# 22 sums of w_down quarters, made on VectorE before and by DRAM-to-DRAM transfers of GpSimd's queue after

## The reference

```
h = rms_norm(x);  proj = h @ w_in           # q, k, v, forget logits, pool input, conv x/B/C, gates
y_a = forgetting_attention(q, k, v) @ w_proj_attn      # 8 heads of 64, causal
y_b = multiscale_pool(u) @ w_proj_pool;  y_c = short_gated_conv(...) @ w_proj_conv
x = x + (gates[0]*y_a + gates[1]*y_b + gates[2]*y_c) @ w_out
a, b = split(rms_norm(x) @ w_gate_up)       # hidden 2816 each
x = x + (silu(a) * b) @ w_down              # w_down: 2816 x 1024: the "way down"
return rms_norm(x)
```

## Time and profile before

| | us |
|---|---|
| median of 3 runs | 773.13 |
| the profiled execution, its own time | 774.61 |
| its span | 772.8 |
| PE busy | 762.9 (99%) |
| DVE (VectorE) busy | 649.2 (84%) |
| ACT (ScalarE) busy | 420.6 (54%) |
| POOL (GpSimd) busy | 18.3 (2%) |
| granted TensorE clock | 0.998 of full speed |

### The profile page before, as it was taken

The page is one execution under the profiler, slowest core; times in us unless marked ns, Lnnn a source line. Parts: engine busy times, 40 slices in busy tenths (PEclk is TensorE's granted clock), DMA queues, the critical chain, the costliest instruction groups (busy, mean ns, idle before and its releaser), DMA issues.

```text
span 772.8 us, 12216 instructions
## 1 busy us (share of the span) xinstructions
PE 762.9 (99%) x4451; PEld 677.7 (88%) x4451; DVE 649.2 (84%) x1041; ACT 420.6 (54%) x712; POOL 18.3 (2%) x41
## 2 busy tenths in 40 slices
PE   8999999999999999999999999999999999999997
PEld 7888888888889999999978888999999998888885
DVE  6788876767798969777777899899999985799997
ACT  5626556647544546455445744555555552655554
POOL 2001101100000000000000000000000000000001
PEclk9999999999999999999999999999999999999999
DMA  8862542323133443344376533333333365353422
GB/s 296 271 220 76 174 105 69 91 54 100 42 105 82 110 121 98 83 110 113 106 265 198 192 98 93 110 111 109 97 100 106 110 196 159 128 172 122 151 96 110
DMA packets 133311, 99.46 MB, mean 129 GB/s; under 512 B 5932, under 2 KB 114532, under 8 KB 133252
## 3 DMA queue, kind: packets, MB, share of 16 engines
q1 hardware_dynamic: 132596, 98.35, 42.2%
q10 hardware_dynamic: 144, 0.26, 0.1%
q0 software_dynamic: 512, 0.07, 0.1%
HBM read 90.21 MB, written 8.39 MB: 128 GB/s over the span
## 4 chain that ended last, share of the span: by engine, by line
PE 96%; DVE 2%; issue 1%; DMA 1%; ACT 0%; POOL 0%; POOLq 0%; DVEq 0%
PE bank L913 10%; PE bank L917 10%; PE bank L915 10%; PE bank L1349 7%; PE bank L1347 7%; PE bank L1345 7%; PE bank L1161 4%; PE bank L1400 4%; PE bank L1159 4%; PE bank L1401 4%; PE bank L1399 4%; PE bank L1157 4%; PE bank L1195 2%; PE bank L1196 2%; PE bank L1197 2%; PE bank L1258 1%
## 5 line engine op out<-in xcount | busy, mean ns | idle before, releaser
L913 PE MATMUL bank<-operands,whi 128*128 128x512 f32 x352 | 138.2, 393 | 0.7 <-DVE wlo L2076 0.7
L917 PE MATMUL bank<-operands,wlo 128*128 128x512 f32 x352 | 137.3, 390 | 0.0
L915 PE MATMUL bank<-operands,whi 128*128 128x512 f32 x352 | 137.2, 390 | 0.0
L2076 DVE TENSOR_TENSOR wlo<-raw,whi 128x1024 fp32r<-128x1024 f32 x61 | 74.3, 1223 | 16.4 <-ACT whi L1465 15.7
L913 PEld LDWEIGHTS bank<-operands,whi 128*128 128x128 f32 x352 | 66.2, 188 | 14.3 <-DVE wlo L2076 1.1
L1465 ACT CAST whi<-raw 128x1024 fp32r<-128x1024 f32 x61 | 63.9, 1052 | 26.9 <-PE bank L917 8.3
L917 PEld LDWEIGHTS bank<-operands,wlo 128*128 128x128 f32 x352 | 66.1, 188 | 13.9
L915 PEld LDWEIGHTS bank<-operands,whi 128*128 128x128 f32 x352 | 66.2, 188 | 13.2
L1349 PE MATMUL bank<-sums_hi,wlo 128*128 128x256 f32 x240 | 68.0, 283 | 0.0
L1347 PE MATMUL bank<-sums_lo,whi 128*128 128x256 f32 x240 | 68.0, 283 | 0.0
L1345 PE MATMUL bank<-sums_hi,whi 128*128 128x256 f32 x240 | 68.0, 283 | 0.0
(11 more groups left out here) (323 smaller groups left out, 2001.8 us busy)
## 6 DMA issues: line engine op xcount, KB each, us to landing
raw<-in_w_in_dram SPq DMA_DIRECT2D x105, 256.0 KB, 3.3
raw<-in_w_gate_up_dram SPq DMA_DIRECT2D x88, 256.0 KB, 3.3
raw<-in_w_down_dram SPq DMA_DIRECT2D x53, 256.0 KB, 3.0
big_x<-in_x_dram SPq DMA_DIRECT2D x8, 512.0 KB, 5.0
tiles<-in_w_out_dram SPq DMA_DIRECT2D x4, 1024.0 KB, 7.4
w_sums<-tiles SPq DMA_DIRECT2D x4, 1024.0 KB, 7.2
raw<-w_sums SPq DMA_DIRECT2D x16, 256.0 KB, 3.1
raw<-in_w_out_dram SPq DMA_DIRECT2D x12, 256.0 KB, 3.7
```

What stands on the lines that cost most here:

```text
L913: nc.tensor.matmul(banks[b][:, 0:width], whi[:, s, w], op(hi + k * S), start=a, stop=False)
L915: nc.tensor.matmul(banks[b][:, 0:width], whi[:, s, w], op(lo + k * S), start=False, stop=False)
L917: mm = nc.tensor.matmul(banks[b][:, 0:width], wlo[:, s, w], op(hi + k * S), start=False, stop=z)
L2076: nc.vector.tensor_tensor(wlo[:, s, :], raw[:, s, :], whi[:, s, :].bitcast(F32), ALU.subtract).then_inc(w_lo, 1)
```

## The change

A new DRAM tensor `down_sums` holds 22 sums: kind 0 is B12 + B11 and kind 1 is B11 + B21 for every r. GpSimd's queue makes them during the pair passes, each kind in two transfers of 1408 rows of 2 KB (2.88 MB): in pass 0 it copies the first addend of kind 0 to DRAM, in pass 1 it waits for that copy and adds the second addend by an accumulating DMA; passes 2 and 3 do the same for kind 1. The transfers stand behind the 4 small DMAs of their pass in the queue. VectorE's `first_sum` and the first addition of `second_sums` are gone. SP waits for both adding transfers ahead of its first w_down load, and loads the sums in place of the second block: kind 0 straight into `chain(r)`, kind 1 into the raw slot. The number and size of its loads stay. For this the load of r = 3 now waits until `used` reaches NU (before, that wait stood in VectorE's `first_sum(3)` and at the load of r = 6). ScalarE waits for the landing in place of VectorE's sum.

```diff
+        down_sums = nc.dram_tensor("down_sums", [2 * FH // 2, D // 2], F32, kind="Internal").ap()
+        def down_sum(kind):
+            return down_sums[kind * R * P:(kind + 1) * R * P, :]
 ... SP
+            sp.wait_ge(down_added, 32)
             for r in range(R):
-                if r == SPARE:
+                if r == SLOTS:
                     sp.wait_ge(used, NU)
-                elif r == SPARE + SLOTS:
+                if r == SPARE + SLOTS:
                     sp.wait_ge(w_lo, NU + 2 * (SPARE - SLOTS) + 2)
-                else:
+                elif r != SPARE:
                     sp.wait_ge(w_lo, NU - SLOTS + r + 1 if r < SLOTS else NU + 2 * (r - SLOTS) + 2)
                 sp.sem_inc(loads_begun, 1)
-                load_down(r, [(2 * r, 1), (2 * r, 0)])
+                load_down(r, [(down_block(2 * r, 1), down_raw(r, 0)),
+                              (down_sum(0)[r * P:(r + 1) * P, :], chain(r))])
...
-                load_down(R + r, [(2 * r, 0), (2 * r + 1, 0)])
+                load_down(R + r, [(down_sum(1)[r * P:(r + 1) * P, :], down_raw(R + r, 0)),
+                                  (down_block(2 * r + 1, 0), down_raw(R + r, 1))])
 ... GpSimd, at the end of each pass i of its loop over the pairs
+                kind, adds = i // 2, i % 2
+                down = w_down.rearrange("(r e p) c -> p r e c", e=2, p=P)
+                to = down_sum(kind).rearrange("(r p) c -> p r c", p=P)
+                if not adds:
+                    pool.dma_start(to, down[:, :, 0, (1 - kind) * HALF:(2 - kind) * HALF]
+                                   ).then_inc(down_copied, 16)
+                else:
+                    pool.wait_ge(down_copied, 16 * kind + 16)
+                    pool.dma_start(to, down[:, :, kind, 0:HALF], accum_op=ALU.add
+                                   ).then_inc(down_added, 16)
 ... ScalarE
                 parts_hi(NU + 2 * r, down_raw(r, 0))
-                act.wait_ge(summed, r + 1)
                 parts_hi(NU + 2 * r + 1, chain(r))
...
-                act.wait_ge(summed, R + 2 * r + 1)
+                act.wait_ge(*landed_down(R + r))
                 parts_hi(u, raw[:, s, 0:2 * HALF], 2)
-                act.wait_ge(summed, R + 2 * r + 2)
+                act.wait_ge(summed, r + 1)
                 parts_hi(u + 2, chain(r))
 ... VectorE: first_sum and its 11 calls are gone, and in second_sums
-                b12, b22 = raw[:, s, 0:HALF], raw[:, s, HALF:2 * HALF]
-                nc.vector.tensor_tensor(b12, b12, b22, ALU.add).then_inc(summed, 1)
+                b22 = raw[:, s, HALF:2 * HALF]
                 nc.vector.tensor_tensor(chain(r), chain(r), b22, ALU.add).then_inc(summed, 1)
```

More of the change, by code:

```diff
@@ L557, in hybrid_block @@
         out_summed, sums_kept = sem("out_summed"), sem("sums_kept")
+        down_copied, down_added = sem("down_copied"), sem("down_added")
         mix_summed, mix_hi, mix_lo = sem("mix_summed"), sem("mix_hi"), sem("mix_lo")
@@ L778, in _, with down_block, load_down @@
                                      ).then_inc(x2_back, 16)
-            def load_down(k, blocks):
+            def down_block(row, c):
+                return w_down[row * P:(row + 1) * P, c * HALF:(c + 1) * HALF]
+            def load_down(k, parts):
                 signal = spare_in if k == SPARE else landed[k % SLOTS]
[L784 to L787, removed]
+                for src, to in parts:
+                    sp.dma_start(to, src).then_inc(signal, 16)
+            sp.wait_ge(down_added, 32)
             for r in range(R):
-                if r == SPARE:
+                if r == SLOTS:
                     sp.wait_ge(used, NU)
-                elif r == SPARE + SLOTS:
+                if r == SPARE + SLOTS:
                     sp.wait_ge(w_lo, NU + 2 * (SPARE - SLOTS) + 2)
-                else:
+                elif r != SPARE:
                     sp.wait_ge(w_lo, NU - SLOTS + r + 1 if r < SLOTS else NU + 2 * (r - SLOTS) + 2)
                 sp.sem_inc(loads_begun, 1)
-                load_down(r, [(2 * r, 1), (2 * r, 0)])
+                load_down(r, [(down_block(2 * r, 1), down_raw(r, 0)),
+                              (down_sum(0)[r * P:(r + 1) * P, :], chain(r))])
             for r in range(R):
@@ L807, in _ @@
                     sp.wait_ge(w_lo, U_3 + ROWS3[q - SLOTS][-1] + 1)
-                    sp.wait_ge(summed, 3 * R + ROWS3[q - SLOTS][-1] + 1)
+                    sp.wait_ge(summed, R + ROWS3[q - SLOTS][-1] + 1)
                 sp.sem_inc(loads_begun, 1)
-                load_down(2 * R + q, [(2 * r + 1, 1) for r in rows])
+                load_down(2 * R + q, [(down_block(2 * r + 1, 1), down_raw(2 * R + q, at))
+                                      for at, r in enumerate(rows)])
             sp.wait_ge(used, U_2 + 6)
@@ L2007, in _ @@
             for rows in ROWS4:
-                act.wait_ge(summed, 3 * R + rows[-1] + 1)
+                act.wait_ge(summed, R + rows[-1] + 1)
                 for at, n in in_one(U_4 + rows[0], len(rows)):
@@ L2656, in parts_lo @@
                                         ALU.subtract).then_inc(w_lo, n)
[L2658 to L2664, removed]
             def gate_rows(stage, j):
@@ L2888, in _ @@
             split_lo("ffn_last", 0, 5)
-            first_sum(0)
             scaled("ffn_last", 1, 20)
             down_lo(0)
-            first_sum(1)
             second_lo(0)
-            first_sum(2)
             down_lo(1)
@@ L2949, in bank_done @@
                     dve.wait_ge(used, u + 1)
-            first_sum(3)
             for r in range(3, R):
                 parts_lo(NU + 2 * r, down_raw(r, 0))
-                if r + 1 < R:
-                    first_sum(r + 1)
-                else:
+                if r == R - 1:
                     second_sums(0)
```

## The result

The changed kernel takes 779.43 us (median of 4 runs, 779.14 to 779.77) against 773.06 us (4 runs): ratio 1.0078, 95% interval 1.0065 to 1.0092, so about 6 us slower. The profiled execution has a span of 777.5 us and a time of its own of 779.31. The profile of the kernel before happened to be 1.5 us over its median, all of it in the first 20 us, so between the traces I compare not spans but how far one runs behind the other at a given matmul.

The account below looks back on a forecast made before the run. TensorE, busy 99% of the span, was taken as the bound. Terms 0 + 0 + 0 + 2.7 us (the late last w_out store) on the median 773.1 gave 775.8 us; range 772.6 to 785, likeliest case 773.1 to 779.

Parts of the forecast that it names:

- rival 3: End of pass 0: GpSimd's ring takes two pieces to one, stores 18.2 us late, total 780 to 787; chance 0.08.
- The sums taken away: Way down: 22 additions, 15.0 us of VectorE, go beside matmuls that ran on; gain 0, at most 0.2 us.
- The loads of the way down: Way down: r = 3's load waits longer but lands before ScalarE's cast; cost 0, upper end 1 us.
- The small DMAs behind the transfers: GpSimd's queue, pass 2: copy and addition, 10 + 25 us, fit in 71.8 us free, so no wait; cost 0.
- rival 2: Pass 2: copy and addition exceed 71.8 us and hold up the small DMAs; 794, to 816 at worst; chance 0.10.
- The tight place: End of pass 0: last w_out store lands late beside GpSimd's transfers; TensorE loses 2.7 us, ends 0 and 4.8.
- Lateness of the store: Last w_out store, end of pass 0: 9.1 us longer with every second piece GpSimd's, less 2.1 us hole: 7.0 late.
- Cover: End of pass 0: 2.0 us margin to ScalarE's write plus 2.3 at unit cv, so 4.3 us of lateness is free.
- weight loads: Passes 1 to 3: 3 us transfers, doubled or trebled, still land within the shortest lead of 13.8 us; cost 0.
- the sign of being wrong altogether: TensorE loses time in passes 1 to 3, where loads had 13.8 us of lead, or gains any in `down`.
- Rival 1: End of pass 0: GpSimd's transfers run thin, stores under 4.3 us late, nothing lost; 773.1 us; chance 0.34.
- Rival 4: Way down: a hidden TensorE wait behind VectorE's 15.0 us makes it faster; 772 at the most; chance 0.04.

Follow-up runs that it names:

- experiment 1: Changed kernel with GpSimd's adding transfers held back until all four w_out stores have landed: 773.42 us, ratio 1.0003.
- experiment 2: Kernel before with only the four GpSimd transfers added, VectorE still making its sums and nobody reading the new tensor: 779.5 us, ratio 1.0084.
- experiment 3: Changed kernel without the four transfers and SP's wait for them, loading plain w_down quarters in place of the sums: 773.68 us, ratio 1.0006.
- experiment 10: Changed kernel with the first adding transfer cut to the sums of r = 0 to 2 in pass 1, the rest in pass 2: 775.45 us, ratio 1.0032.
- experiment 5: Changed kernel with ScalarE's wait for the w_out stores moved behind its first writes of pass 0: 780.23 us, ratio 1.0089.
- experiment 8: Changed kernel with GpSimd's adding transfers held back only until the third w_out store has landed: 779.15 us, ratio 1.0083.
- experiment 9: Changed kernel with plain copies in place of the two adding transfers, sums left out: 781.11 us, ratio 1.0101.

## Why the prediction was right, and where it was not

**Direction, place and range** came out: 779.4 in 772.6 to 785.0, slower, at the end of pass 0, behind ScalarE's wait for the last w_out store, with a wait of TensorE on unit cv's low part. Experiments 1, 2 and 3 show it from three sides. The size did not: 775.8 was forecast, and 779.4 lies past 779, where the terms' own ends stopped. The range held because it had been drawn out to 785 for rival 3.

**The sums taken away: 0, right.** Experiment 3 gives 1.0006 with the relief alone. Of the 15.0 us, 11.3 show in VectorE's busy time. An addition is shown with 0.68 us, but the next instruction starts 0.60 us behind it (692.28 and 692.88 in the trace before), which makes some 1.8 us of the difference; the rest I have not traced. (The waits of TensorE before were five in four rows, three of them in the middle, not four; the sum and the conclusion stay.)

**The loads of the way down: 0, right.** Load 3 went out at 667.17 and its cast came at 671.60 without a wait.

**The small DMAs behind the transfers: 0, right.** Copy and first addition took 13.2 and 25.9 us (I had 10 and 25), 39 of the 71.8 that were free, so rival 2 is excluded. In quieter places an addition took 21 us and a copy 12 to 13.

**The tight place: 2.7 forecast, 6.3 measured.** This is the step that was mis-sized, in two of its terms and by one that I left out.

- Lateness of the store: 7.0 forecast, 7.8 measured. That the sum is near is luck, since two errors cancelled. I had a hole of 2.1 us between copy and addition; it was 5.3 us (last copy pieces at 86.3, first adding pieces behind 91.6), so that only 3.6 us of the store's own time were left (88.08 + 7.1 = 95.2). At every second piece and equal time for a piece, as I had it, it would have been 3.6 us late. The pieces did alternate, but an adding piece holds an engine 1.8 times as long as one of the store's. Rival 3 had GpSimd's queue take twice the share, for a wrong reason (two pieces to one) and with no hole; its 18.2 us of lateness did not come. The Trainium skill ("DMA: Bandwidth & Descriptors", queues, rings and completion order) says that an engine turns between rings by packets. The trace agrees, if a record is a packet: one record of 2.05 KB for one of SP's, be it 2 KB (128 to 128) or 512 B (332 to 333). The two rows a turn that rival 3 made of it did not come out for the addition, whose records hold one row.
- Cover: 4.3 forecast, 2.6 measured (experiment 10). The 2.0 us up to ScalarE's write were right. The 2.3 at unit cv cover only unit cv. Behind it ScalarE and VectorE make q, k, the parts of cb and cc and the softmax of the first scores in an unbroken row, with 0.58 us of idle, up to the second scores.
- The load of cb: left out. I gave weight loads doubled or trebled time, from 3 us, against a lead of 13.8 us, from a load of pass 1. The one behind the last store took 6.9 us already before the change; it had some 17 us of lead and took 22.8, 3.3 times as long. It alone costs as much (experiment 5), 1.1 us of it beyond the store. I had named time lost in passes 1 to 3, against the loads' lead, as the sign of being wrong altogether: for this load, and for that of cc in experiment 8, it came.

With these: 7.8 - 2.0 = 5.8, + 1.1, - 0.6 = 6.3.

**Rival 1** (nothing lost) had its decision point at a landing of 101.1 by the earlier trace's time, 99.5 by the later one's; the store landed at 103.0. With the right cover of 2.6 us the point lies at 97.9, by the later trace's time. **Rival 4** is excluded by experiment 3.

## What to carry to other kernels

Cover for a late transfer is the least idle time along the whole in-order chain behind it, up to the last engine that bounds the kernel, not the slack at the first thing that chain delivers. A DMA that nobody waits for is free only where no transfer with a short lead shares the DMA engines with it; the queues took turns piece by piece here, so a bulk transfer of large pieces made loads of 512 B pieces 3 to 4 times slower, so it wants a wait that holds it out of the crowd (experiment 1 gave everything back). And before work is taken from an engine, see that somebody waits for it: 15 us of additions on VectorE were worth nothing here, and no version of this change ran faster than the kernel before.

## What was not expected of the hardware

- The stall was followed by some 3.5 us at half the granted clock, and filling it kept the clock up, but the time did not change (779.43 and 779.68): the slow stretch lay within a wait for late data.
- An adding transfer's first pieces came more than 3 us after its issue instruction had ended (issued 86.36 for 2.02 us, first data records behind 91.6). It is not the adding: the plain copy of experiment 9, issued at 86.27, moved none before 91.5 either, while the copy of pass 0 (72.83) moved data before 75. The cause stays open.
- A plain DRAM-to-DRAM copy moved 4.0 KB a record, the adding one 2.05 KB, both from rows of 2 KB; beside the copy the store took 16.7 us, beside the addition 14.9.
- Two queues with work shared the engines record for record, so that a queue of 512 B pieces got 21% of their time beside one of 2 KB adding pieces, which had 91%.
